# The last attention of a two-block fp32 transformer: small sums on GpSimd, first scores between the query transposes, one gate from the exponential

## The reference

```python
def sink_softmax(scores, sink):
    m = sink
    for s in scores:
        m = jnp.maximum(m, jnp.max(s, axis=-1))
    exps = [jnp.exp(s - m[..., None]) for s in scores]
    den = jnp.exp(sink - m)
    for e in exps:
        den = den + jnp.sum(e, axis=-1)
    return tuple(e / den[..., None] for e in exps)

def attn_mixer(h_lat, h_ctx, w_in, q_g, k_g, sink, w_out, need_ctx):
    ...
    q = rms_norm_2(q.reshape(b, t, AT_HEADS, AT_HEAD_DIM), q_g)
    k = rms_norm_2(k.reshape(b, t, AT_KV_HEADS, AT_HEAD_DIM), k_g)
    ...
    ql = apply_rope(ql, cos, sin) * scale
    kl = apply_rope(kl, cos, sin)
    ...
    p_loc, p_ctx = sink_softmax((s_loc, s_ctx), sink_f[None, None, :, :, None])
    ...
    y_lat = (o * jax.nn.silu(zl)) @ w_out
```

## Time and profile before

| | us |
|---|---|
| runs shown, median of 3 (lowest, highest) | 1968.23 (1966.79, 1968.38) |
| the profiled execution: its time | 1967.3 |
| its span | 1965.1 |
| PE busy | 1927.1 (98%) |
| DVE busy | 1303.8 (66%) |
| ACT busy | 904.7 (46%) |
| POOL busy | 52.4 (3%) |

### The profile page before, as it was taken

The page is one execution under the profiler, slowest core; times in us unless marked ns, Lnnn a source line. Parts: engine busy times, 40 slices in busy tenths (PEclk is TensorE's granted clock), DMA queues, the critical chain, the costliest instruction groups (busy, mean ns, idle before and its releaser), DMA issues. The chain is left out here.

```text
span 1965.1 us, 31270 instructions
## 1 busy us (share of the span) xinstructions
PE 1927.1 (98%) x12652; PEld 1618.6 (82%) x12652; DVE 1303.8 (66%) x2407; ACT 904.7 (46%) x1635; POOL 52.4 (3%) x78
## 2 busy tenths in 40 slices
PE   7999999999999999999999999999999999999998
PEld 5788668889888888898689899998887788888867
DVE  5547777857886665667766777675566464555886
ACT  4446863325423232355764655443443432234685
POOL 0000000001000000000000000000000000001000
PEclk9999999999999999999999999999999999999999
DMA  8322016543545455443139455554311133432411
GB/s 314 117 85 100 18 52 233 179 160 108 193 175 207 177 193 191 166 150 108 54 136 336 172 191 196 177 186 161 119 54 54 65 118 119 150 128 86 150 45 44
DMA packets 53583, 278.39 MB, mean 142 GB/s; under 512 B 4536, under 2 KB 19128, under 8 KB 24512
## 3 DMA queue, kind: packets, MB, share of 16 engines
q1 hardware_dynamic: 47168, 265.50, 37.5%
q10 hardware_dynamic: 6128, 10.03, 1.7%
q0 software_dynamic: 144, 0.85, 0.1%
HBM read 274.26 MB, written 2.11 MB: 141 GB/s over the span
## 5 line engine op out<-in xcount | busy, mean ns | idle before, releaser
L640 PE MATMUL ps<-t 128*128 128x512 f32 (+1 forms) x1936 | 665.2, 344 | 2.4 <-DVE t L2035 2.4
L642 PE MATMUL ps<-t 128*128 128x512 f32 (+1 forms) x1936 | 659.0, 340 | 0.0
L641 PE MATMUL ps<-t 128*128 128x512 f32 (+1 forms) x1936 | 659.0, 340 | 0.0
L2035 DVE TENSOR_TENSOR t<-t 128x1024 fp32r<-128x1024 f32 (+2 forms) x370 | 413.9, 1159 | 153.1 <-ACT t L1386 152.2
L1386 ACT ACTIVATE t<-t 128x1024 fp32r<-128x1024 f32 (+3 forms) x376 | 358.3, 1001 | 194.3 <-PE ps L642 142.6
L640 PEld LDWEIGHTS ps<-t 128*128 128x128 f32 x1936 | 363.6, 188 | 52.5 <-issue 5.1
L642 PEld LDWEIGHTS ps<-t 128*128 128x128 f32 x1936 | 363.6, 188 | 42.5
L641 PEld LDWEIGHTS ps<-t 128*128 128x128 f32 x1936 | 363.7, 188 | 41.8 <-issue 0.7
L2021 DVE TENSOR_TENSOR t<-t 128x256 f32<-128x256 f32 (+9 forms) x622 | 227.9, 386 | 134.3 <-ACT t L1770 31.2
L2030 DVE SCALAR_TENSOR_TENSOR t<-t 128x256 f32<-128x256 f32 (+4 forms) x372 | 272.8, 765 | 34.1 <-ACT t L1491 21.9
L1491 ACT ACTIVATE t<-ps 128x512 f32<-128x512 f32 (+2 forms) x239 | 112.9, 494 | 289.2 <-PE ps L642 187.3
(11 more groups left out here) (191 smaller groups left out, 2278.4 us busy)
## 6 DMA issues: line engine op xcount, KB each, us to landing
t<-in_panels SPq DMA_DIRECT2D x231, 1024.0 KB, 4.9
t<-in_panels SPq DMA_DIRECT2D x12, 768.0 KB, 4.4
t<-in_panels SPq DMA_DIRECT2D x16, 512.0 KB, 3.6
t<-in_window ACTq DMA_DIRECT2D x4, 768.0 KB, 4.5
t<-gates_between ACTq DMA_DIRECT2D x4, 512.0 KB, 4.8
t<-in_panels SPq DMA_DIRECT2D x1, 1088.0 KB, 5.0
t<-in_ctxT SPq DMA_DIRECT2D x1, 1024.0 KB, 6.7
t<-in_xT SPq DMA_DIRECT2D x1, 1024.0 KB, 8.9
```

The costliest lines, as they stand in the source:

```text
L640: e.matmul(o, hi[:, k, w], xh[:, c0:c1], start=k == 0, stop=False)
L641: e.matmul(o, hi[:, k, w], xl[:, c0:c1], start=False, stop=False)
L642: t = e.matmul(o, lo[:, k, w], xh[:, c0:c1], start=False, stop=k == p.nk - 1)
L2035: e.tensor_tensor(p.half(p.split(wlo), a), p.half(raw[p.slot], a), p.half(p.split(whi), a).bitcast(F32), ALU.subtract).then_inc(*up(ve, (" ...
```

## The change

- **GpSimd** (`sink_units`, new) takes over in the last attention's softmax: sink plus maximum (`("sink", "A", i)`), the sum of the denominator (`("den", "A", i)`), and both parts of the gated chunks 0 to 6 (a cast copy and a difference of 128 x 256). Chunk 7 stays with ScalarE and VectorE.
- **Panel `atz` 3**'s remainder is taken by GpSimd too (`POOL_PANELS`), in two instructions of 128 x 1024.
- **The query transposes** go to banks 4 to 7, twice: chunks 0 to 3 first, then the scores of unit 0, then chunks 4 to 7, then the scores of unit 1.
- **Gate panel 3** goes to banks 6 and 7. ScalarE takes exp(-x) in place of the sigmoid, GpSimd adds 1, VectorE takes the reciprocal (128 x 256, twice) and multiplies. On VectorE it stands in turn 2, after the maximum of unit 2.
- **ScalarE** loads the exponential's table between its copies of query chunks 3 and 4.
- **VectorE** scales unit 1 before the maximum of unit 2; from then on the order in a turn is as before.

The diff, without the parts that only move lines into functions:

```diff
-POOL_PANELS = [("uq", 0, 0), ("uq", 1, 0), ("atkv", 0)]
+POOL_PANELS = [("uq", 0, 0), ("uq", 1, 0), ("atkv", 0), ("atz", 3)]
...
-                for c in range(8):
-                    o = bank(("aqT", c))
-                    if c % 4 == 0:
-                        e.wait_ge(*done(("q heads", c // 4)))
...
-                softmax("A", at_units(), aPT, lambda i: gate(3, (4, 5)) if i == 1 else None)
+                def query_features(c0):
+                    for c in range(c0, c0 + 4):
+                        o = bank(("aqT", c), (4 + c % 4,))
+                        if c == c0:
+                            e.wait_ge(*done(("q heads", c // 4)))
+                        for tile in range(2):
+                            t = e.transpose(o[:, tile * 128:tile * 128 + 128], aqtok[:, tile, c * 128:c * 128 + 128], ident)
+                        t.then_inc(*up(pe, ("full", ("aqT", c))))
+
+                query_features(0)
+
+                def among(i):
+                    if i == 0:
+                        query_features(4)
+                    if i == 1:
+                        gate(3, (6, 7))
+
+                softmax("A", at_units(), aPT, among)
...
-                        elif i3 % 2 == 0 and i3 >= 2:
-                            gate_hi(i3 // 2 - 1)
...
-                        e.activation(sz[:, c, :], banks(("atz", c))[:, 0:256], ACT.Sigmoid).then_inc(*up(se, ("asig", c)))
+                        f, m = (ACT.Sigmoid, 1.0) if a < 3 else (ACT.Exp, -1.0)
+                        e.activation(sz[:, c, :], banks(("atz", c))[:, 0:256], f, scale=m).then_inc(*up(se, ("asig", c)))
...
                 for c in range(8):
+                    if c == 4:
+                        own()
+                        e.activation(root[:, :], epst[:, :], ACT.Exp).then_inc(*up(se))
...
+                def scale(i):
+                    u, par = units[i - 1], (i - 1) % 2
+                    r = rs[:, spot[i - 1]]
+                    e.wait_ge(*done(("den" if u["sink"] is not None else "exp", s, i - 1)))
+                    e.reciprocal(r, r).then_inc(*up(ve))
...
                 for i in range(n_u + 4):
+                    early = s == "A" and i == 2
+                    if early:
+                        scale(i)
...
-                            own()
-                            tt(st[2][:, spot[i]], m, u["sink"], ALU.add, ("sink", s, i))
...
-                        if u["sink"] is not None:
-                            tt(r, r, st[2][:, spot[i - 1]], ALU.add)
...
-                        if i3 % 2 and i3 >= 3:
-                            gate_lo(i3 // 2 - 1)
...
                 def gate(a):
                     for c in range(2 * a, 2 * a + 2):
-                        e.wait_ge(*done(("asig", c)))
+                        e.wait_ge(*done(("asig" if a < 3 else "one more", c)))
+                        if a == 3:
+                            e.reciprocal(sz[:, c, :], sz[:, c, :]).then_inc(*up(ve))
+                            own()
...
                 def among_units(i):
-                    if i == 1:
+                    if i == 2:
                         gate(3)
...
+            def sink_units():
+                units = at_units()
+                spot = spots(units)
+                for i in range(len(units) + 3):
+                    if i == 2:
+                        for c in (6, 7):
+                            e.wait_ge(*done(("asig", c)))
+                            e.tensor_scalar(sz[:, c, :], sz[:, c, :], 1.0, None, ALU.add).then_inc(*up(po, ("one more", c)))
+                    if 1 <= i <= len(units):
+                        r, es = ast[1][:, spot[i - 1]], ast[2][:, spot[i - 1]]
+                        e.wait_ge(*done(("exp", "A", i - 1)))
+                        e.tensor_tensor(r, r, es, ALU.add).then_inc(*up(po, ("den", "A", i - 1)))
+                    if i < len(units):
+                        m, es = ast[0][:, spot[i]], ast[2][:, spot[i]]
+                        e.wait_ge(*done(("max", "A", i)))
+                        e.tensor_tensor(es, m, units[i]["sink"], ALU.add).then_inc(*up(po, ("sink", "A", i)))
+                    if i % 2 == 0 and 4 <= i < 18:
+                        c = i // 2 - 2
+                        e.wait_ge(*done(("az", c)))
+                        e.tensor_copy(aYh[:, c, :], sz[:, c, :]).then_inc(*up(po))
+                        e.wait_ge(po.sem, po.n)
+                        e.tensor_tensor(aYl[:, c, :], sz[:, c, :], aYh[:, c, :].bitcast(F32), ALU.subtract).then_inc(
+                            *up(po, ("aylo", c)))
...
+            lo(at["atz", 3])
+            sink_units()
```

More of the change, by code:

```diff
@@ L2201, in softmax, with maximum @@
                 n_u, spot = len(units), spots(units)
+                def maximum(i):
+                    u, par = units[i], i % 2
+                    both = psum[:, 2 * par:2 * par + 2, :]
+                    e.wait_ge(*done(("full", ("s", s, i))))
+                    m = nm[:, spot[i]]
+                    mv = m.rearrange("p (g x) -> p g x", g=2)
+                    if u["bias"]:
+                        e.wait_ge(*u["bready"])
+                        near = st[2][:, spot[i]]
+                        for g in range(2):
+                            v = banks(("s", s, i, g))[:, 256:512]
+                            e.tensor_tensor_reduce(v, v, u["bias"][g], 1.0, NEG, ALU.add, ALU.max, near[:, g:g + 1]).then_inc(*up(ve))
+                        e.tensor_reduce(mv, both[:, :, 0:256].rearrange("p g (x n) -> p g x n", x=1), AX.X, ALU.max,
+                                        negate=True).then_inc(*up(ve))
+                        own()
+                        stt(m, near, -1.0, m, ALU.mult, ALU.min, ("max", s, i))
+                    else:
+                        e.tensor_reduce(mv, both.rearrange("p g (x n) -> p g x n", x=u["xs"]), AX.X, ALU.max, negate=True).then_inc(
+                            *up(ve, ("max", s, i)))
+                    if u["rms"] is not None:
+                        own()
+                        tt(mv, mv, u["rms"], ALU.mult, ("max", s, i))
+                    if u["sink"] is not None:
+                        own()
+                        tt(m, m, u["nsink"], ALU.min, ("max", s, i))
@@ new lines, in scale @@
+                def scale(i):
[3 more added lines that the diff above has]
+                    e.reciprocal(r, r).then_inc(*up(ve))
+                    own()
+                    w = 512 // u["xs"]
+                    for g in range(2):
+                        for x in range(u["xs"]):
+                            v = work[:, 2 * par + g, x * w:x * w + w]
+                            c = g * u["xs"] + x
+                            ts(v, v, r[:, c:c + 1], None, ALU.mult, None, ("p", s, i - 1))
@@ L2246, in softmax @@
+                        maximum(i)
+                    if 1 <= i <= n_u and not early:
+                        scale(i)
                     if i >= 4 and units[i - 4]["yh"] is not None:
```

23 lines of the change are left out of this document (removed).

## The result

The changed kernel takes 1973.33 us (median of 7 runs, 1972.82 to 1974.14), the kernel before 1967.51 on the same chip (7 runs, 1966.79 to 1968.38): a ratio of 1.0029 with a 95% interval of 1.0019 to 1.0038. It is 5.8 us slower. The forecast was 1972.7 with a range of 1969.6 to 1976.0, and it was made as +4.5 on a median of 1968.2.

What follows compares the result with a forecast made beforehand. VectorE was taken to bound the steady turns, with TensorE 98% busy and waiting ahead of the softmax. Terms 4.0 + 3.45 - 3.2 + 0.8 - 0.5 = +4.5 on 1968.2 gave 1972.7 us, range 1969.6 to 1976.0.

Steps and rivals of the forecast that it cites:

- the rival with the clock: TensorE's clock falls in its 5.4 us wait for the banks; forecast plus 1 to 2.25, about 1974.5 us; chance 0.30.
- GpSimd's allowance of 0.8: Steady turns: GpSimd's copy and low part may delay the next denominator, 0 to 1.6 us over the stage; +0.8 taken.
- B: Query transposes wait for gate panel 2's banks behind the held rope; scores of unit 2 at 1890.85, not 1886.82: +4.0.
- A: Last rope: GpSimd's split of panel 3 holds the port shared with VectorE, so the rope ends 3.6 us late.
- unheld rope: Rival at the last rope: VectorE is not held, or not for long; sum +1.0, 1969.2 us; chance 0.14.
- C: Unit 1's denominator stands behind gate chunk 7 on GpSimd; maximum of unit 2 starts 0.9 us later than its scores allow.
- D: Two VectorE reciprocals of 1.75 us between maxima of units 2 and 3 delay unit 2's transposes; with C, +3.45.
- E: Eleven steady turns: VectorE is relieved, TensorE's 2.94 us a turn is next; 32.3 us, not 35.57: -3.2.
- F: From unit 13's transposes to the end of unit 15's values: the chain loses two short sums and a chunk's part, -0.5.
- a faster kernel: Rival: neither rope nor reciprocals are late, 2.9 us of reciprocals hidden; sum -2.8, 1965.4 us; chance 0.05.
- GpSimd as the bound of the turns: Rival in the steady turns: denominators take some 0.35 us longer in each of 14 turns; +5, 1977.5 us; chance 0.06.

## Why the prediction was right, step by step

The direction was right and the time 0.6 us off, but part of that is luck. The change itself was forecast at +4.5 and measured at +5.8; the time came closer only because the kernel before took 1967.5 beside it, 0.7 less than the 1968.2 I started from. And errors in the sum have opposite signs: the rival with the clock came true as well, for 2.7 us that are not in it, GpSimd's allowance of 0.8 in the steady turns was nothing, and B was some 0.4 too dear.

- **A, the rope held by GpSimd: shown.** Forecast 3.6 us late. The two products behind the rope start at 1880.63 against 1876.30, and 0.8 of that lies ahead: 3.5. The split alone gives the same lengths (4.73 and 3.52), and with the split back the six take 2.23 again. 2.2 of the 3.5 us are lost in the seven instructions of the tile before and 1.3 in the last tile's. This is the Trainium skill's rule (SBUF — State Buffer, "Who interferes with whom") of an exclusive lock; the trace agrees, with 3.51 us for six instructions of 2.23.
- **B, the transposes behind the banks: right, a little too large.** Forecast +4.0; at full clock it is about 3.6 (6.3 less the 2.7 that the filled wait gives back). With an unheld rope I had put it at +0.45, and with the split back it is +0.2. That the banks make the held rope dearer is shown by the version with other banks (+3.1, with a shorter half rate). That the order of before would have been cheaper beside a held rope is not: there the split costs 7.0 in this stretch, more of it at half rate.
- **The clock, a rival with 0.30: it came true beside the forecast.** The two didn't exclude each other. The half rate cost 2.7 us where my bound was 2.25 (2.2 and 1.9 in the two other traces with this wait); I had let it last 4.5 us, and it lasted 6.8, to 1887.12. Every one of the seven runs has a mean clock of 0.996 or 0.997, against 0.999 or 1.000 in all but one of the 70 runs of the kernel before beside the experiments. The Trainium skill (TensorE: Matmul & The Clock Gate, "Why this matters for your kernels") had said that such a gap brings the clock down; the trace agrees for 5.29 us, and I should have given its rule more than 0.30.
- **C, the denominator behind the additions: right, a little small.** An addition took 0.87 us, not 0.5, just over the upper bound of 0.81. The maximum of unit 2 starts 2.64 us behind its scores, and 1.38 with the denominator first: 1.26 late, not 0.9.
- **D, two reciprocals: right.** 1.75 each, the maxima 5.8 us apart; C and D together +3.6 for +3.45. What was missed is that the clock falls again at TensorE's waits for the reciprocals (2.56 us, and 2.35 where the work between runs at full rate). In after that costs nothing more: the slower work only shortens the second wait to 0.77 us. In the milder versions it costs 1.3 to 1.6 us.
- **E, the steady turns: right, without the allowance.** 2.94 us each, -3.2, as forecast. The 0.8 for GpSimd was 0: 0.20 a small sum and 0.73 the low part are the cheap ends of my bounds, and 0.40 for the copy is near its own.
- **F, the end: right.** -0.6 for -0.5.

By stretches the sum is +6.1, by medians +5.8. The rivals of an unheld rope and of a faster kernel fall with A and D, GpSimd as the bound of the turns with E.

Open: why the runs with the split back on VectorE differ by 4.4 us. Their time goes roughly with their mean clock, but only the fastest one has a trace. Not all of such a spread need come from this stage. In the traces the last matmul of gate panel 2, ahead of what the experiments touch on TensorE, starts between 1873.8 and 1876.8, and with the small sums alone on GpSimd (1876.63) the clock was at half from 15.0 to 18.4 us. Not tried: the split on GpSimd at another place, with no rope beside it.

## What to carry over

An engine that is 3% busy is no free place for work if it shares a port with the engine that others wait for: look at what stands on VectorE in those microseconds, and not at GpSimd's share. Where a change leaves TensorE a wait longer than any that the trace shows at full clock, count the half rate behind the wait too; removing one such wait can just move the loss to the next, so take away all of them before judging a part. And look for a form of the function that needs no division: a tanh in the exponential's place gave the same gate without the reciprocals.

## What was not expected of the hardware

- The clock fell at waits much shorter than the 5.4 us of the forecast: 2.89 us with the other banks, 2.55 with the filled wait, and at the second of two waits of 2.56 and 2.35, with 2.4 us of work between, when the split was back on VectorE. There, and with the other banks (2.55), the first of the two had left it full, so the same length did it in one place and not in another. Waits of 1.41 and 1.81 (the split back) left it full. It fell in the second half of a wait or up to 1.2 us behind it, when TensorE was at work again, and stayed at half for 3.4 us at the least and 10.2 at the most (the split alone on before).
- An addition of 1 on GpSimd, with one input of 128 x 256, takes 0.87 us, no less than an operation with two inputs (0.81).
- An fp32 matmul of 128 x 256 is two records of some 0.22 us each (22 records in 4.91 us for 11 matmuls).
- The tanh brought no table load beside the exponential's.
